# Reordering and operand placement at five norms and three products of a fused two-block kernel

## What is computed

```python
def first_block(x, p, ...):
    x = x + s5_mixer(rmsnorm(x, norm_mix), ..., ssm_w_glu)          # ends in a gated product
    x = x + sqrelu_mlp(rmsnorm(x, norm_ffn), mlp_w1, mlp_w2)
    gate = sigmoid(rmsnorm(x, norm_ple) @ ple_gate_w)
    x = x + (p @ ple_w) * gate
    return rmsnorm(x, norm_final)

def mixer_stream(...):                     # in both layers
    gates = sigmoid(zgate)                 # four gates of width 1024
    ys = stack([y_four, y_conv, y_gqa, y_diff])
    return sum(gates * ys, axis=branch) @ w_out

# a layer: x = x + g_m * mixer_stream(modulate(rms_norm(x)));  x = x + g_f * swiglu(modulate(rms_norm(x)))
# the end: rms_norm(x, final_norm)
```

## Time and profile before

| | us |
|---|---|
| three runs, median (lowest to highest) | 2161.28 (2160.78 to 2166.43) |
| the profiled execution, its own time | 2168.67 |
| its span | 2166.8 |
| PE busy | 1976.3 |
| POOL busy | 1082.1 |
| DVE busy | 1018.8 |
| ACT busy | 747.4 |
| mean granted TensorE clock, share of full speed | 0.946 |

### The profile page before, as it was taken

One profiled execution on the slowest core, in us unless ns is written; L12 is line 12 of the kernel. 1 busy time (PEld: TensorE's weight loads), 2 busy tenths in 40 slices (PEclk: granted clock), 3 DMA queues, 4 the chain that ended last, 5 costly groups with the idle time before them and its releaser, 6 DMA issues.

```text
span 2166.8 us, 32878 instructions
## 1 busy us (share of the span) xinstructions
PE 1976.3 (91%) x13805; PEld 1742.4 (80%) x13805; DVE 1018.8 (47%) x1690; ACT 747.4 (34%) x1208; POOL 1082.1 (50%) x565
## 2 busy tenths in 40 slices
PE   3986899988899999989988999999898998888998
PEld 3755899977798778968767888888797897888997
DVE  7853554125483576483236111112558767453114
ACT  2213254323223542262222222222243535334442
POOL 7003588746344544304333444444366751776885
PEclk9788899988899999999998999999898999998998
DMA  5344677786512214102322323322254241544552
GB/s 145 99 150 156 219 242 236 253 277 226 163 58 78 70 32 132 45 28 88 129 85 78 98 72 104 97 85 87 82 156 146 70 136 30 166 158 151 178 174 80
DMA packets 285735, 274.01 MB, mean 126 GB/s; under 512 B 6459, under 2 KB 283461, under 8 KB 285333
## 3 DMA queue, kind: packets, MB, share of 16 engines
q1 hardware_dynamic: 282164, 265.94, 38.5%
q10 hardware_dynamic: 2688, 4.86, 0.8%
q0 software_dynamic: 736, 1.12, 0.3%
HBM read 265.86 MB, written 4.19 MB: 125 GB/s over the span
## 4 chain that ended last, share of the span: by engine, by line
PE 81%; DVE 12%; ACT 3%; issue 2%; DMA 2%; POOL 1%; DVEq 0%; SPq 0%; ACTq 0%; POOLq 0%
PE gb L2290 17%; PE gb L2291 17%; PE gb L2292 17%; PE gb L1324 3%; PE gb L1325 3%; PE gb L1326 3%; PE gb L1530 3%; PE gb L1529 3%; PE gb L1528 3%; PE mb L2427 1%; PE mb L1079 1%; DVE mx L1108 1%; PE mb L611 1%; PE mb L1134 1%; POOL wl L2278 1%
## 5 line engine op out<-in xcount | busy, mean ns | idle before, releaser
L2278 POOL TENSOR_TENSOR wl<-raw,wh 128x1024 fp32r<-128x1024 f32 (+3 forms) x452 | 985.8, 2200 | 952.3 <-ACT wh L730 951.7
L730 ACT CAST wh<-raw 128x1024 fp32r<-128x1024 f32 (+3 forms) x452 | 418.7, 937 | 794.2 <-PE gb L2292 406.2
L2290 PE MATMUL gb<-xh,wh 128*128 128x256 f32 (+1 forms) x1920 | 632.9, 330 | 43.3 <-DVE pr L1892 16.0
L2291 PE MATMUL gb<-xl,wh 128*128 128x256 f32 (+1 forms) x1920 | 628.8, 327 | 0.0
L2292 PE MATMUL gb<-xh,wl 128*128 128x256 f32 (+1 forms) x1920 | 628.2, 327 | 0.0
L2290 PEld LDWEIGHTS gb<-xh,wh 128*128 128x128 f32 x1920 | 372.4, 194 | 79.8 <-issue 36.0
L2291 PEld LDWEIGHTS gb<-xl,wh 128*128 128x128 f32 x1920 | 372.4, 194 | 28.9
L2292 PEld LDWEIGHTS gb<-xh,wl 128*128 128x128 f32 x1920 | 371.7, 194 | 29.4
L1324 PE MATMUL gb<-wh,xh 128*128 128x256 f32 x608 | 174.7, 287 | 1.4 <-POOL wl L2278 1.4
L1325 PE MATMUL gb<-wh,xl 128*128 128x256 f32 x608 | 173.1, 285 | 0.0
L1326 PE MATMUL gb<-wl,xh 128*128 128x256 f32 x608 | 173.0, 284 | 0.0
(11 more groups left out here) (425 smaller groups left out, 3116.4 us busy)
## 6 DMA issues: line engine op xcount, KB each, us to landing
raw<-in_w_in SPq DMA_DIRECT2D x62, 1024.0 KB, 5.3
raw<-in_w_ada SPq DMA_DIRECT2D x48, 1024.0 KB, 6.5
raw<-in_w_ffn SPq DMA_DIRECT2D x44, 1024.0 KB, 5.1
raw<-in_mlp_w SPq DMA_DIRECT2D x32, 1024.0 KB, 6.4
raw<-in_w_ffn SPq DMA_DIRECT2D x16, 768.0 KB, 4.6
raw<-in_w_ffn SPq DMA_DIRECT2D x16, 640.0 KB, 4.2
raw<-in_ssm_w_glu SPq DMA_DIRECT2D x8, 1024.0 KB, 6.8
raw<-in_w_out SPq DMA_DIRECT2D x8, 1024.0 KB, 5.0
```

The lines of the kernel that those rows point to most:

```text
L730: nc.scalar.copy(split_half(wh, p, j, h), raw_half(p, it, j, h)).then_inc(hi_ready, 1)
L2278: nc.gpsimd.tensor_tensor(split_half(wl, p, j, h), raw_half(p, it, j, h), split_half(wh, p, j, h).bitcast(F32), ALU.subtract)\
L2290: nc.tensor.matmul(o, H[:, k, :], XH, start=st, stop=False)
L2291: nc.tensor.matmul(o, H[:, k, :], XL, start=False, stop=False)
```

## The change

It has four parts.

1. The product called `glu` starts without `lead=THREE`: PE takes half-block after half-block, each as soon as it has its `wl`, and `ada_select` follows block 0 as before.
2. In `gemm_act`, `split_first=False` moves the splits of the next phase's first block from behind the last but one block of a phase to behind `squares_act`. It is given for `glu` and `mlp2` (norms 0 and 1). It is also given for the last phase of layer 1, which has no phase behind it and so no splits.
3. Norms 0, 1, 5 and 8 use `rsqrt_beside` with the temporaries in bank 1 of `gb`, and the last step writes the diagonal (`wide`). Norm 2 has its temporaries in bank 1 too, instead of bank 3.
4. Of the operand of `wo`, tiles 0 to 3 go into `brh` and `brl`, which branch 3 does not use, and are made two blocks sooner: on ACT before block 5, on DVE at pair 2 in front of its L1892. Tiles 4 and 5 stay at pair 3.

```diff
-        def gemm_act(act, p, evac, before=None, tail=None):
+        def gemm_act(act, p, evac, before=None, tail=None, split_first=True):
...
+                    late = tail is not None and i >= p.n - 2
+                    if late:
                         evac(it, j)
-                        if it * p.body + j == p.n - 1:
+                        if i == p.n - 2 and split_first:
+                            for h in range(2):
+                                split_hi(act, nxt, h)
+                        if i == p.n - 1:
                             tail()
+                            for g in ([] if split_first else [ahead(p, it, j - 1)]) + [nxt]:
+                                if g is not None:
+                                    for h in range(2):
+                                        split_hi(act, g, h)
+                        continue
...
-        def rsqrt_beside(T1, ms, y, yp, t):
+        def rsqrt_beside(T1, ms, y, yp, t, wide=None):
...
+                if i == 2 and wide is not None:
+                    t, y = (a.unsqueeze(2).to_broadcast([P, a.shape[1], P]) for a in (t, y))
+                    T1.add(v.scalar_tensor_tensor(wide, t, 1.5, y, ALU.add, ALU.mult))
+                    return
...
+            if n in (0, 1, 5, 8):
+                T1.add(nc.vector.tensor_scalar(rs[:, 0, 0:nt], total, 1.0 / count, eps, ALU.mult, ALU.add))
+                T1.wait()
+                rsqrt_beside(T1, rs[:, 0, 0:nt], rs[:, 1, 0:nt], *(gb[:, 1, 448 + 8 * i:448 + 8 * i + nt]
+                                                                   for i in range(2)), wide=dg[:, 0:nt, :])
...
-            gemm_pe(pe, q["wo"], T, X2(T), first_use(pe, s_ml, 8 * l), lead=THREE)
+            gemm_pe(pe, q["wo"], T, XM(T), first_use(pe, s_ml, 8 * l), lead=THREE)
...
-                    nc.scalar.mul(xh[:, k, 0:T], mix[:, k, 0:T], 0.5).then_inc(s_mh, 1)
+                    nc.scalar.mul((brh if k < 4 else xh)[:, k, 0:T], mix[:, k, 0:T], 0.5).then_inc(s_mh, 1)
...
+                if (it, j) == (1, 1):
+                    mixed_hi(0, 4)
                 if (it, j) == (1, 3):
-                    mixed_hi(0, 6)
+                    mixed_hi(4, 6)
...
+                        if b == 3 and pair == 2:
+                            mixed_lo(0, 4)
                         if b == 3 and pair == 3:
-                            mixed_lo(0, 6)
+                            mixed_lo(4, 6)
...
-            gemm_act(act, p_m2, lambda it, j: None, tail=lambda: squares_act(act, 1, sqr))
+            gemm_act(act, p_m2, lambda it, j: None, tail=lambda: squares_act(act, 1, sqr), split_first=False)
...
-            gemm_pe(pe, p_glu, SEQ, X, operand(0), selection(0, 0), THREE)
+            gemm_pe(pe, p_glu, SEQ, X, operand(0), selection(0, 0))
```

23 lines of the change are left out of this document (13 added, 10 removed).

## The result

The changed kernel takes 2150.74 us (median of 9 runs, 2145.64 to 2156.12), the kernel before, run beside it, 2165.02 (9 runs, 2159.17 to 2168.70). The ratio is 0.9941, 95% interval 0.9923 to 0.9959: 12.8 us saved by the ratio, 14.3 by the medians, against a forecast of 21.6. In three later comparisons the same kernel had 0.9912, 0.9914 and 0.9916. Over all runs, the medians are 2167.5 (135 runs) and 2150.3 (26 runs), 17.2 us apart. One run of before, of 3673.74 us, is left out of the 135 as a slow one.

A forecast was written before the change was run, and what follows sets the result against it. PE, busy 1976.3 of 2166.8 us, bounds the kernel, so only its idle and lower-clock stretches can shrink. Terms 6.4, 1.7, 3.7, 2.3, -0.6, 6.0 and 2.1 sum to 21.6: 2161.28 becomes 2139.7, range 2131 to 2152.

The forecast's parts named there:

- the term of layer 0: PE starts `wo` 4.5 us sooner (up to 6.2 in the first case), plus clock kept: 6.0, ends 3 and 8.
- the phases behind run as before: Behind each place: phases are only earlier, PE busy without a gap, and the loads move along.
- What holds the small steps, and what part 3 buys: At the norms: SBUF-only DVE steps pass once per POOL instruction; with one operand in PSUM they take 0.2 us.
- `glu`: Start of `glu`: PE starts at 188.9 instead of 195.31, no later half-block waits; gain 6.4 us, ends 5.0 and 6.6.
- the lower clock in `glu`: `glu`: PE could stay at the lower level between half-blocks, 32 us lost, giving 2172; chance 0.02.
- late weights: Behind `glu`: load stream without slack, gains at `glu`, norms 0 and 1 (11.8) lost to landings, 2151.5; chance 0.07.
- Norms 0, 1 and 5: Spread sooner by 1.7 and 3.7 us at norms 0 and 1, the modulation block late next; norm 5's root 2.3.
- the rival of the held roots: Roots: first steps take the lock, norm 5 gains nothing, norms 0 and 1 little; 2146, chance 0.03.
- Layer 1: Held subtractions bring a new 1.8 us wait at block 7; `wo` starts 2.1 us sooner, ends -1 and 7.
- The rival without the new wait: Layer 1: a subtraction slips between POOL instructions, `wo` starts about 1915, 3.5 to 5 more; 2135, chance 0.12.
- I carry the difference over to the median: Predicted time: profiled execution is 7.4 above the median of three runs, so 2161.28 - 21.6 = 2139.7.
- The ends: Range of the sum: all upper ends give 32 (2129), all lower ends 11 (2151); low end 2131, high 2152.

The follow-up runs named there:

- part 1 alone: The kernel before with only the `glu` start without the lead, and norm 2's temporaries in bank 1: 2158.85 us (12 runs), ratio 0.9949.
- only_norms: The kernel before with parts 2 and 3 alone: 2157.10 us (12 runs), ratio 0.9948.
- again_2: The changed kernel once more with no edit, for its third trace: 2146.91 us (4 runs), ratio 0.9914 to the kernel before.
- mix_sooner: The changed kernel with the four mixed tiles made one block sooner still: 2144.13 us (6 runs), ratio 0.9900 to the kernel before.
- both_more: The changed kernel with spread before modulation block at norms 0 and 1, mixed tiles a block sooner, norm 8's root as before: 2141.70 us, ratio 0.9883.

## Why the prediction was right in its places and wrong in its size

The step that failed in the sum is the term of layer 0, in its part for the clock, and with it the sentence that the phases behind run as before; the step that failed in the predicted time is besides the base that I carried it over to.

- **What holds the small steps, and what part 3 buys.** Right: no step over 0.17 us in PSUM, 0.85 to 2.27 for four steps in SBUF at the same place.
- **`glu`.** Right: 6.4 forecast, 6.6 us at norm 0 with part 1 alone, no wait at the half-blocks behind, the clock back at its upper level at 192.4 us, 4.5 behind PE's start. So the rivals of the lower clock in `glu` and of late weights fell.
- **Norms 0, 1 and 5.** Right, and for the reason given: 1.7, 3.7, 2.3 against 1.9, 4.3 and 2.0 (only_norms against before); the rival of the held roots fell. Of the 4.2 at norm 1 only 1.9 are idle time, though; 2.2 come from work that PE did at the upper level instead of the lower (11.6 us busy at the lower level from norm 0 to norm 1 before, 6.7 after), which the prediction did not name. Late next was the landing of the modulation block, as the spread in front of it showed.
- **Layer 0.** The wait fell by 4.5 us, as forecast. The other 1.5 rested on the clock being kept over a standstill of 3.4 us, and I read that from one fall in one trace. Three of the four traces of after lost the clock; in again_2 it stayed. The rows of after and of again_2 (length, then busy PE, PEld, DVE, ACT, POOL, PEclk, DMA share, GB/s), that of after first:

```profile
1096.00:1097.00 1.00, 0.00 (x0) 0.00 (x0) 1.00 (x2) 0.00 (x0) 1.00 (x2) 0.98 1.08 384
1097.00:1098.00 1.00, 0.12 (x1) 0.15 (x1) 0.96 (x2) 0.00 (x0) 1.00 (x1) 0.50 0.93 329
1103.00:1104.00 1.00, 1.00 (x4) 0.77 (x4) 0.00 (x0) 0.00 (x0) 0.00 (x0) 0.61 0.39 137
```

and again_2, its first matmul of `wo` in the timeline and the same view:

```profile
1098.55 0.47 PE L2317 MATMUL gb<-brh,wh 128*128 128x512 f32 x1 [3.43 <-DVE pr L1919]
```

```profile
1098.00:1099.00 1.00, 0.45 (x2) 0.44 (x3) 0.96 (x2) 0.00 (x0) 1.00 (x1) 1.00 0.62 219
```

The standstill is 3.43 us in both. In the first the level is 1.2 GHz from 1097.0 to 1103.8 and the stretch from norm 3 to norm 4 is 2.1 us shorter than before; in again_2 it stays at 2.4 GHz and the stretch is 6.6 shorter (263.1 against 256.5). The 6.0 came only in the second case, one trace of four, and even there 2.9 us of the 6.6 are the clock elsewhere between norms 3 and 4. This is the term that was mis-sized: 6.0 forecast, 2.1 in the first pair and 3.5 between the means. Its wait fell as forecast (idle 26.7 to 22.2 us), but the clock, forecast to give 1.5, took 1.6: PE was busy at the lower level for 15.8 us of the stretch before and 19.4 after, since the level now fell just before PE started and was low for the 5.9 us behind. The other eight traces with part 4 have the same standstill of 3.43 us, and all lost the clock, two of them for 6.8 us and six for 3.4; in all eleven it fell 2.2 to 4.6 us after PE stopped. Of twelve, the level was kept in one.
- **Layer 1.** The mechanism was right to the tenth (a wait of 1.8 forecast in front of block 7, 1.76 measured; 2.1 at the start of `wo`, 2.3 measured), and 1.2 was left by norm 7. The rival without the new wait fell; mix_sooner, which has none, gives 3.7 from norm 6 to norm 7, less than the 5.6 to 7.1 that the rival had.
- **"Behind each place the phases run as before, only earlier."** Wrong in both directions: 3.4 us more were gained from norm 1 to norm 3, and 0.6 more than norm 8's own 0.6 were lost in front of it. Both are for the most part the clock. From norm 1 to norm 3 PE's idle time is 20.5 us before and 19.7 after, its time at the lower level 31.7 and 25.8. The first place is the start of `ple`: before, its matmuls run 0.21 us apart until 487.3, while after, the level is back at 468.9 and they run 0.12 apart from the first on. Before and then after:

```profile
484.56 0.41 PE L2290 MATMUL gb<-xh,wh 128*128 128x256 f32 x1
484.77 0.41 PE L2291 MATMUL gb<-xl,wh 128*128 128x256 f32 x1
...
470.53 0.28 PE L2317 MATMUL gb<-xh,wh 128*128 128x256 f32 x1
470.65 0.28 PE L2318 MATMUL gb<-xl,wh 128*128 128x256 f32 x1
```

From norm 7 to norm 8 the lower level holds 5.8 us of PE's work instead of 4.5: 5.8 to 6.0 in every trace with part 4 but mix_sooner and both_more, and 4.5 or 4.6 in every trace without it. So a shorter wait moves the places where the clock comes back behind it. That makes up for layer 0 in the sum, so that 20.8 against 21.6 is a better match than its terms deserve: it is luck in part.
- **"I carry the difference over to the median."** This failed for the predicted time. The three runs shown, 2161.28, lay low: 135 runs of before have a median of 2167.5, and the profiled execution that I took for 7.4 us slow was at 1.2 above it. Of the 10.6 us between 2139.7 and the 2150.3 of all runs of after, 6.2 are this base (3.7 by the 2165.02 of the first comparison). The other 4.4 are the gain itself, 17.2 against 21.6. The table gives 20.5 between the means of the five and the four traces (front plus norm 8: 187.4 + 1968.1 against 188.3 + 1946.7), where each front can be 12 us off. The four comparisons by medians gave 14.3, 19.9, 20.9 and 15.3. Single runs scatter by 4.8 us (before) and 4.3 (after) about their means, so a difference between five and four of them is uncertain by 3.1 (one standard error), and the 20.5 does not contradict the 17.2. The rival of a slow trace of before, 13 to 17, was thus wrong in its reason behind `glu` and near in its number. What of the 4.4 us is chance and what the terms, these runs don't tell.
- **The ends.** The upper ends add up to 31.3 and not 32, and the upper end of layer 0's first case is 6.5 and not 6.2. Neither changes the forecast.

## What to carry over

Cost a wait at its place, and keep apart from it what the clock may add. PE's idle time fell by what was forecast, within 0.4 us, at `glu` with norm 0, at norm 5 and in front of `wo` in both layers (8.1, 2.4, 4.5 and 1.7 against 8.1, 2.3, 4.5 and 2.1); at norm 1 it fell by 1.9 against 3.7. The clock was kept over the shorter standstill in one execution of twelve. To compare single traces, split each stretch into idle time, time at the lower level and the rest. Where GpSimd works beside a chain of tiny VectorE steps, give each step an operand in PSUM before moving anything that lets GpSimd start sooner: at norm 0 the second alone cost 1.7 us. And take the base from many runs when the forecast is under 1%: three runs were 6 us off.
